# Sample attention: one page of each of four batches in a step, each batch in its own quarter of the array's columns

## The chip, the cores and the metric

The kernel runs on one core of a Trainium2 chip. The metric is the device time of one execution in microseconds (us), the median of several runs.

## The reference

One decoder layer is computed for two groups of tokens that share all weights: a prompt of 512 tokens, and a sample group of 8 batches with 4 new tokens each (32 tokens). The layer is a half-step feed-forward block, a mixer of a state-space branch (S5) and a sparse attention branch, and a second half-step feed-forward block. The change touches the attention of the sample group only:

```
# per batch b of 8: 4 queries, 8 heads of 64; past of 1024 keys = 8 pages of 128, found through page_table
score = indexer(q_idx, k_idx)                      # over 1024 + 4 keys
idx   = top_k(score, 256)
s     = q . k[idx] / 8 + bias[bucket(distance), head]
out   = softmax(s) @ v[idx]                        # then @ w_att_proj, gated by sigmoid(gate_att)
```

The keys and values of the past lie in pages of a pool in HBM, one page being 128 keys by 512 numbers in f32 (256 KB). The kernel does not gather the 256 chosen keys. It computes scores for all 1056 columns (1024 past keys and 32 new ones), adds a large negative number where a key is not chosen, and multiplies the resulting probabilities with all the values.

## The kernel before, in words

Each engine has its own instruction stream, written out by hand, and the streams meet only at semaphores. TensorE ("PE") does all matmuls and transposes. A transpose is called a turn below. PSUM has eight banks of 512 f32 columns; `ps[:, b, :]` is bank b.

The sample attention stands between the end of the prompt's attention and the projection of both. It works in two groups g of four batches. A batch has 32 rows (8 heads by 4 queries), so the four batches of a group fill the 128 partitions of PSUM: batch 4g + c has the partitions 32c to 32c + 31. The output partitions of a matmul tell which quarter of the array's columns it uses. A stationary operand is here 128 rows (or, for the new tokens, 32) by 32 columns.

**K phase of a group.** Eight steps i = 0 to 7. A step takes four pages of keys, 1 MB, which are two steps a batch. `k_turn(g, i)` (L1009) turns the four pages with 16 transposes of 128x128 into banks 3 to 6. ScalarE (L1406) copies banks 3 and 4 and VectorE (L1917) banks 5 and 6 into `pgT`, which has two buffers. `k_score(g, i)` (L1018) multiplies the step's keys with the batch's queries, which lie in `qbd` (block-diagonal over heads, four blocks j of 128 rows): four matmuls of 128x32 by 128x512, all into the same 32 partitions, accumulated over j. After each second step, four small matmuls (L1022) make the scores against the 32 new tokens. The order on TensorE is turn i, score i - 1, and after the steps 2, 3, 5 and 6 one block `ga_half` of another computation, the attention gate's projection (16 passes through the helper's line L555), which was put there as filling. Two more such blocks follow the last score. `k_turn(g, i)` waits until both copies of step i - 1 are done, since the banks are single; `k_score(g, i)` waits until those of step i are done.

**Softmax.** VectorE adds the bias and takes the maximum, ScalarE makes the exponentials (L1411), TensorE turns them (L1054, L1055), ScalarE copies them to `ptS` (L1416, L1417): `ptS[:, k, :]` holds the 128 keys of page k of all four batches, in 128 columns.

**V phase of a group.** Eight steps again; a step has four pages of values, used as they are: four matmuls (L1062) of 128x32 by 128x512 into the 32 partitions of one batch in bank 5. After each second step one matmul (L1066) adds the values of the new tokens. After the steps 4 and 5 stands a `ga_half`. VectorE then scales the result (L1927), and TensorE gathers it by token (through L555).

**Pages.** There are four slots `kpage[r]` of four pages each; step i uses slot i % 4. Two queues load them: SyncE ("SP") issues pages 0 and 1 of a slot, GpSimd ("POOL") pages 2 and 3, in the order K steps 0 to 7, V steps 0 to 7 of group 0, then of group 1 (`page_load`, L425). Each load waits on the semaphore `kv_used`, which counts steps done: in the K phase VectorE raises it once a step is turned, in the V phase TensorE does with a step's last matmul. The page number is read from the page table in SBUF just before each DMA.

**After the stage.** SyncE loads w_att_proj (L530, four blocks of 512 KB into the memory of the page slots) once the seventh V step of group 1 is done, and then w_out (L538). TensorE needs all of w_att_proj for the projection (through L555), which follows on the gathering of the result. The gate's weights are loaded on ScalarE's queue (L1389), two blocks ahead.

Of the kernel before, what the change touches and what calls it, by code (L numbers as in the profile page):

```python
# [34 lines left out]
P = 128  # L35
D = 1024
DK = D // P
SEQ, NB, NS = 512, 8, 4
NT = SEQ + NB * NS
# [63 lines left out]
def build(nc, t, out):  # L103

    ctx = ExitStack()
    with ctx:
        def sb(name, shape, dt=F32):
            return ctx.enter_context(nc.sbuf_tensor(name, shape, dt))

        def sem(name):  # L110
            return ctx.enter_context(nc.semaphore(name))
# [16 lines left out]
        qbd = sb("qbd", [P, 4, NB, HEADS * NS])  # L128
        ident = sb("ident_sb", [P, P])
# [9 lines left out]
        pt_sb = sb("pt_sb", [1, NB * NPAGE], I32)  # L139
        ps = ctx.enter_context(nc.psum_tensor("ps", [P, 8, 512], F32))  # L140
# [22 lines left out]
        ktok, vtok = kvtok[:, 0], kvtok[:, 1]  # L163
        qT, kT = qkT[:, 0], qkT[:, 1]
# [55 lines left out]
        def v(k):  # L220
# [20 lines left out]
        kpage = [[wflat[:, a:a + 512] for a in (1024, 1536, 3392, 3904)], [biasmem[:, 512 * k:512 * k + 512] for k in range(4)],  # L241
                 [biasmem[:, 512 * k:512 * k + 512] for k in range(4, 8)], [wflat[:, a:a + 512] for a in (0, 512, 2368, 2880)]]
# [7 lines left out]
        pgT = uv[:, :, :].rearrange("p a n -> p (a n)")[:, 0:4096].rearrange("p (b j n) -> p b j n", b=2, j=4)  # L250
        sms = big[:, base:base + NKEY]
        pes = big[:, base + 1056:base + 1056 + NKEY]
        ptS = big[:, base + 2112:base + 2112 + 9 * P].rearrange("p (k n) -> p k n", k=9)
# [32 lines left out]
        s = {n: sem(n) for n in (  # L286

            "gain_row_in", "par_in", "sample_const_in",
            "kidx_in", "bias_in", "att_w_in", "shift_out", "toep_in", "u_out", "u_in", "kidx_out", "kv_out", "res_out",

            "mm_done", "evac",

            "unit_done", "hi_done", "lo_done", "ffn_ev", "silu_done", "acth_done", "act_ready",

# [125 lines left out]
        def page_load(eng, first, src, g, c, i, r):  # L420

            eng.wait_ge(s["kv_used"], i * 4 + (16 * g + 8 * c + r + 1))
            for k in range(first, first + 2):
                pg = eng.value_load(pt_sb[0:1, bass.ds(i * 16 + (32 * g + 4 * r + k), 1)], min_val=0, max_val=src.shape[0] - 1)
                eng.dma_start(kpage[r][k], src[bass.ds(pg, 1), :, :].rearrange("a p d -> p (a d)")).then_inc(kv_in[first // 2][r], 16)  # L425

        def page_loads(eng, first):
# [123 lines left out]
        def _(pe):  # L551
# [130 lines left out]
            for h in range(2):  # L682
                ins = pe.matmul(ps[:, 6 + h, :], ones[0:1, :], gain_row[:, 512 * h:512 * h + 512], start=True, stop=True)
# [18 lines left out]
            for k in range(2):  # L702
                ins = pe.matmul(ps[0:HEADS, 6 + k, 0:320], relb, ohp[0:NBKT, 320 * k:320 * k + 320], start=True, stop=True)
            ins.then_inc(s["shift_mm"], 1)
            for c in range(2):
                ins = pe.transpose(ps[:, 5, P * c:P * c + P], s0raw[:, c, :], ident[:])
# [3 lines left out]
            for r in range(8):  # L710
                c, g4 = r // 4, r % 4
# [7 lines left out]
                for q in range(4):  # L719
                    ins = pe.transpose(ps[:, (r + 2) % 8, P * q:P * q + P], wb[:, c, 4 * g4 + q, :, :].rearrange("p t j -> p (t j)"), ident[:])  # L720
# [21 lines left out]
            for r in range(4):  # L742
                if r >= 2:
                    pe.wait_ge(s["lag_kernels_out"], r - 1)
                for q in range(4):
                    gp = 4 * r + q
                    for c, y in enumerate((yre, yim)):
                        for h in range(2):
                            sl = slice(64 * h, 64 * h + 64)
                            ins = pe.matmul(ps[0:16, 4 + 2 * (r % 2) + h, P * q:P * q + P], bbar[sl, c, gp, :], y[sl, gp, 0:CH, :],  # L750
                                            start=(c == 0), stop=(c == 1), skip_group_check=True)
# [12 lines left out]
            for h in range(IH):  # L764
                ins = pe.transpose(ps[:, 6, 32 * h:32 * h + 32], qis4[:, h, :, :].rearrange("p r d -> p (r d)"), ident[0:32, 0:32])
# [36 lines left out]
            for q in range(4):  # L802
                for g4 in range(4):
                    gp = 4 * q + g4
                    for h in range(2):
                        for c in range(2):
                            ins = pe.matmul(ps[64 * h:64 * h + 64, 2 * q + c, UC * g4:UC * g4 + UC], gb[:, c, gp, 64 * h:64 * h + 64],
                                            uch[:, 2 * gp + h, :], start=True, stop=True)
# [55 lines left out]
            for c in range(2):  # L864
                pe.transpose(ps[:, 0, P * c:P * c + P], fin_s[:, c, :, :].rearrange("p b g -> p (b g)"), ident[:])
                ins = pe.transpose(ps[0:GP, 0, 256 + P * c:384 + P * c], fin_p[:, c, :], ident[:])
# [30 lines left out]
            for both in range(NB // 2):  # L897
# [7 lines left out]
                if both % 2:  # L905
                    g = both // 2
                    pe.wait_ge(s["sample_relu"], g + 1)
                    for k, (c0, c1) in enumerate(cols):
                        ins = pe.matmul(ps[0:32, 5 + k, 0:c1 - c0], wsel[:, g, :], rls[:, c0:c1], start=(g == 0), stop=(g == 1))
# [3 lines left out]
            for b, (c0, c1) in enumerate(cols):  # L913
                ins = pe.matmul(ps[:, b, 0:c1 - c0], rbexp, ohs[:, c0:c1], start=True, stop=True)
# [84 lines left out]
            def k_turn(g, i):  # L999
                n = 8 * g + i  # L1000
                for half in range(2):
                    pe.wait_ge(kv_in[half][i % 4], 32 * (4 * g + i // 4 + 1))
                if i:

                    pe.wait_ge(s["k_out_act"], n)
                    pe.wait_ge(s["k_out_dve"], n)
                for j in range(4):
                    for k in range(4):
                        ins = pe.transpose(ps[:, 3 + j, P * k:P * k + P], kpage[i % 4][k][:, P * j:P * j + P], ident[:])  # L1009
                    ins.then_inc(s["k_turned"], 1)  # L1010

            def k_score(g, i):
                n = 8 * g + i
                b, q = 4 * g + i // 2, slice(32 * (i // 2), 32 * (i // 2) + 32)
                pe.wait_ge(s["k_out_act"], n + 1)
                pe.wait_ge(s["k_out_dve"], n + 1)
                for j in range(4):
                    ins = pe.matmul(ps[q, i % 2, :], qbd[:, j, b, :], pgT[:, n % 2, j, :], start=False, stop=(j == 3), skip_group_check=True)  # L1018
                ins.then_inc(s["k_scored"], 1)
                if i % 2:  # L1020
                    for j in range(4):
                        ins = pe.matmul(ps[q, 2, 0:32], qbd[:, j, b, :], kT[:, j, SEQ:NT], start=False, stop=(j == 3), skip_group_check=True)  # L1022
                    if i == 7:
                        ins.then_inc(s["sample_scores"], 1)

            def ga_half(m):

# [7 lines left out]
            for g in range(2):  # L1035
                if g:
                    pe.wait_ge(s["sample_biased"], g)
                    pe.wait_ge(s["sample_probs_out"], g)
                    pe.wait_ge(s["sample_values_out"], g)
                for k, (c0, c1) in enumerate(cols):  # L1040
                    pe.matmul(ps[:, k, 0:c1 - c0], tok_row[:, g, :], sels[:, c0:c1], start=True, stop=False, skip_group_check=True)
                for i in range(8):
                    k_turn(g, i)
                    if i:
                        k_score(g, i - 1)
                    if i in GA_AFTER_K:
                        ga_half(8 * g + GA_AFTER_K.index(i))
                k_score(g, 7)
                ga_half(8 * g + 4)
                ga_half(8 * g + 5)  # L1050
                pe.wait_ge(s["ga_ev"], 8 * g + 6)
                pe.wait_ge(s["sample_exp"], g + 1)
                for k in range(NPAGE):
                    pe.transpose(ps[:, 6 + k // 4, P * (k % 4):P * (k % 4) + P], pes[:, P * k:P * k + P], ident[:])  # L1054
                pe.transpose(ps[0:32, 5, 0:P], pes[:, PAST:NKEY], ident[:]).then_inc(s["sample_probs_turned"], 1)  # L1055
                pe.wait_ge(s["sample_probs_out"], g + 1)
                for i in range(8):
                    q = slice(32 * (i // 2), 32 * (i // 2) + 32)
                    for half in range(2):
                        pe.wait_ge(kv_in[half][i % 4], 32 * (4 * g + 2 + i // 4 + 1))  # L1060
                    for k in range(4):
                        ins = pe.matmul(ps[q, 5, :], ptS[:, 4 * (i % 2) + k, q], kpage[i % 4][k], start=(i % 2 == 0 and k == 0),  # L1062
                                        stop=False, skip_group_check=True)
                    ins.then_inc(s["kv_used"], 1)
                    if i % 2:
                        ins = pe.matmul(ps[q, 5, :], ptS[0:32, 8, q], vtok[0:32, 4, :], start=False, stop=True, skip_group_check=True)  # L1066
                        if i == 7:
                            ins.then_inc(s["sample_values"], 1)
                    if i in GA_AFTER_V:
                        ga_half(8 * g + 6 + GA_AFTER_V.index(i))  # L1070

            pe.wait_ge(s["sample_values_out"], 2)
            for j in range(4):
                ins = acc(ps[:, 6, 32 * j:32 * j + 32], [(osel[:, g, P * j:P * j + P], row_tok[:, g, :]) for g in range(2)])
# [5 lines left out]
            for i in range(DK):  # L1080
                if i >= 2:
                    pe.wait_ge(s["att_ev"], i - 1)
                for h in range(2):
                    ins = acc(ps[:, 4 * (i % 2) + h, 0:HALF], [(attw[k][:, P * i:P * i + P], attT[:, k, h * HALF:(h + 1) * HALF]) for k in range(4)])
# [13 lines left out]
            for k in range(5):  # L1098
                m = P if k < 4 else 32
                ins = pe.matmul(ps[0:m, 0, k:k + 1], running[3][:, P * k:P * k + m], ones[:, 0:1], start=True, stop=True)  # L1100
# [898 lines left out]
```

## Time and profile before

| | |
|---|---|
| median of 3 runs | 1613.44 us (1612.92 to 1614.85) |
| profiled execution | 1611.19 us |
| its span | 1609.5 us |
| TensorE busy | 95% of the span |
| VectorE, ScalarE, GpSimd busy | 38%, 28%, 16% |
| DMA | 148.00 MB, mean 92 GB/s |

The profile is of one execution. Times in it are microseconds from the start of the span. "PE" is TensorE's matmuls, "PEld" its weight loads, "DVE" VectorE, "ACT" ScalarE, "POOL" GpSimd, "SP" SyncE; a "q" behind a name means its sequencer or queue. The ends of matmuls are modelled, so spacings of starts tell more than durations. PEclk is the clock that TensorE was granted, as a share of 2.4 GHz.

### The profile page before, as it was taken

What the parts mean: (1) busy time and instruction counts of PE and PEld (TensorE: products, weight loads), DVE (VectorE), ACT (ScalarE), POOL (GpSimd) and SP (SyncE); (2) the same over time, 40 slices, a digit from 0 to 9 for tenths busy, and PEclk for the clock granted to TensorE, in tenths of its full rate; (3) what the DMA queues carried; (4) which work ended last, traced back from release to release, by engine and by line L of the source; (5) the groups of instructions that cost most, each with busy time, mean ns of one, the idle gap of its engine ahead of it and who ended that gap; (6) DMA issues with size and microseconds to landing.
All of it is one profiled execution on the core that took longest, in us unless ns stands there. A gap on an engine that the chain in (4) does not pass through costs nothing. (4 is left out here: it accounts for less than half of the span.)

```text
span 1609.5 us, 26811 instructions
## 1 busy us (share of the span) xinstructions
PE 1535.1 (95%) x10350; PEld 1314.5 (82%) x10350; DVE 608.5 (38%) x957; ACT 452.6 (28%) x647; POOL 263.7 (16%) x458
## 2 busy tenths in 40 slices
PE   7999999999899899899998999999999999999996
PEld 6999999999867677577666544635899999999996
DVE  3333343333522574155553101102454343343344
ACT  4332222122402201354543110110243222221234
POOL 3000000882003096011333111110000000000000
PEclk9999999999989999999999999999999999999998
DMA  9522323322215621721114446433233233223321
GB/s 135 143 83 79 88 82 92 89 82 72 68 23 104 107 63 17 145 62 43 53 53 148 153 138 202 144 133 105 56 89 92 79 92 92 82 88 92 87 66 61
DMA packets 228744, 148.00 MB, mean 92 GB/s; under 512 B 29730, under 2 KB 211818, under 8 KB 228667
## 3 DMA queue, kind: packets, MB, share of 16 engines
q1 hardware_dynamic: 195904, 118.06, 25.2%
q0 software_dynamic: 7088, 19.65, 5.3%
q10 hardware_dynamic: 25674, 9.25, 3.5%
q8 instruction: 51, 0.84, 0.2%
q14 instruction: 27, 0.21, 0.0%
HBM read 139.62 MB, written 6.12 MB: 91 GB/s over the span
## 5 line engine op out<-in xcount | busy, mean ns | idle before, releaser
L1597 DVE TENSOR_TENSOR w_low<-wraw,w_high 128x1024 fp32r<-128x1024 f32 x144 | 178.9, 1243 | 320.3 <-ACT w_high L1129 320.3
L575 PE MATMUL ps<-hn_high,w_high 128*128 128x272 f32 x1408 | 292.6, 289 | 2.9 <-DVE w_low L1597 2.9
L575 PE MATMUL ps<-hn_high,w_low 128*128 128x272 f32 x1408 | 292.4, 289 | 0.0
L575 PE MATMUL ps<-hn_low,w_high 128*128 128x272 f32 x1408 | 291.3, 288 | 0.0
L1129 ACT ACTIVATE w_high<-wraw 128x1024 fp32r<-128x1024 f32 x144 | 152.4, 1060 | 447.7 <-PE ps L575 443.7
L575 PEld LDWEIGHTS ps<-hn_high,w_high 128*128 128x128 f32 x1408 | 222.6, 189 | 3.1 <-issue 3.0
L575 PEld LDWEIGHTS ps<-hn_low,w_high 128*128 128x128 f32 x1408 | 222.4, 189 | 0.0
L575 PEld LDWEIGHTS ps<-hn_high,w_low 128*128 128x128 f32 x1408 | 220.7, 190 | 0.0
L575 PE MATMUL ps<-act_high,w_high 128*128 128x272 f32 x832 | 173.5, 290 | 5.3 <-DVE w_low L1597 3.5
L575 PE MATMUL ps<-act_high,w_low 128*128 128x272 f32 x832 | 172.8, 289 | 0.0
L575 PE MATMUL ps<-act_low,w_high 128*128 128x272 f32 x832 | 172.2, 288 | 0.0
L575 PEld LDWEIGHTS ps<-act_high,w_high 128*128 128x128 f32 x832 | 131.1, 189 | 6.3 <-issue 3.9
L575 PEld LDWEIGHTS ps<-act_low,w_high 128*128 128x128 f32 x832 | 131.1, 189 | 0.0
L575 PEld LDWEIGHTS ps<-act_high,w_low 128*128 128x128 f32 x832 | 130.6, 190 | 0.0
L1488 POOL TENSOR_TENSOR kvtok<-qkT,apow 128x256 f32<-128x256 f32 x68 | 51.2, 783 | 261.8 <-DVEq L1781 253.9
L555 PE MATMUL ps<-wslot,hn 128*128 128x256 f32 (+3 forms) x416 | 85.0, 369 | 1.1 <-ACT uv L1294 1.1
L555 PEld LDWEIGHTS ps<-wslot,hn 128*128 128x128 f32 (+1 forms) x416 | 66.7, 179 | 19.2 <-issue 6.2
L555 PE MATMUL ps<-uv,wslot 128*128 128x272 f32 x256 | 65.5, 399 | 5.3 <-ACT sg L1368 5.3
L555 PEld LDWEIGHTS ps<-uv,wslot 128*128 128x128 f32 x256 | 46.1, 190 | 23.4 <-issue 15.9
L940 PE MATMUL ps<-hn,wslot 128*128 128x272 f32 x256 | 65.0, 399 | 0.0
L555 PE MATMUL ps<-hn,big 128*128 128x272 f32 x256 | 62.9, 399 | 1.0 <-ACT qkT L1394 0.5
L555 PEld LDWEIGHTS ps<-hn,big 128*128 128x128 f32 x256 | 47.3, 190 | 17.6 <-issue 6.7
(328 smaller groups left out, 1746.4 us busy)
## 6 DMA issues: line engine op xcount, KB each, us to landing
wraw<-in_w_ffn_in SPq DMA_DIRECT2D x88, 512.0 KB, 3.9
wraw<-in_w_ffn_out SPq DMA_DIRECT2D x32, 512.0 KB, 3.9
wslot<-in_w_in SPq DMA_DIRECT2D x16, 512.0 KB, 4.0
wraw<-in_w_ffn_out SPq DMA_DIRECT2D x16, 384.0 KB, 3.4
wslot<-in_w_in SPq DMA_DIRECT2D x4, 1024.0 KB, 6.1
wslot<-in_cache_k POOLq DMA_DIRECT2D x16, 256.0 KB, 3.9
wslot<-in_w_s_glu SPq DMA_DIRECT2D x16, 256.0 KB, 3.0
wslot<-in_cache_k SPq DMA_DIRECT2D x16, 256.0 KB, 4.0
```

The source lines that it names most:

```text
L555: ins = pe.matmul(dst, a, b, start=(k == 0), stop=(k == len(pairs) - 1), **kw)
L575: ins = pe.matmul(ps[:, bank + h, 0:HALF], a[:, w_at, k, :], x[:, lo_at(k) if x is x_lo else k, h * HALF:(h + 1) * HALF], start=(k == 0 an ...
L940: ins = pe.matmul(ps[:, 4 * slot + h, 0:HALF], slot_block(slot, k), hn[:, k, h * HALF:(h + 1) * HALF], start=(k == 0), stop=(k == DK - 1), ...
L1129: act_e.activation(wh[:, j % 2, :, :], wraw[:, j, :, :], ACT.Copy).then_inc(s["hi_done"], 1)
L1488: ins = pool.tensor_tensor(o, a, b, ALU.mult)
L1597: return dve.tensor_tensor(o, a, b, op)
```

## The change

A step now takes page i of each of the four batches of the group, in place of four pages of one batch. The page number is read from another place of the page table (L424). The number of pages, steps, loads and semaphores stays. In `k_score` each of the four blocks j has now four matmuls of 128x32 by 128x128, one for each batch, into four different sets of 32 partitions. In the V phase the four matmuls of a step go to four different sets of 32 partitions, with 512 columns as before. The matmuls of the new tokens stand together behind the last step of the phase. `tile_position` names the quarter of the array's columns.

```diff
@@ page_load
-                pg = eng.value_load(pt_sb[0:1, bass.ds(i * 16 + (32 * g + 4 * r + k), 1)], min_val=0, max_val=src.shape[0] - 1)
+                pg = eng.value_load(pt_sb[0:1, bass.ds(i * 4 + (32 * g + 8 * k + r), 1)], min_val=0, max_val=src.shape[0] - 1)
@@ k_turn (only the name of the loop's variable)
-                    for k in range(4):
-                        ins = pe.transpose(ps[:, 3 + j, P * k:P * k + P], kpage[i % 4][k][:, P * j:P * j + P], ident[:])
+                    for c in range(4):
+                        ins = pe.transpose(ps[:, 3 + j, P * c:P * c + P], kpage[i % 4][c][:, P * j:P * j + P], ident[:])
@@ k_score
-                b, q = 4 * g + i // 2, slice(32 * (i // 2), 32 * (i // 2) + 32)
...
                 for j in range(4):
-                    ins = pe.matmul(ps[q, i % 2, :], qbd[:, j, b, :], pgT[:, n % 2, j, :], start=False, stop=(j == 3), skip_group_check=True)
+                    for c in range(4):
+                        ins = pe.matmul(ps[32 * c:32 * c + 32, i // 4, P * (i % 4):P * (i % 4) + P], qbd[:, j, 4 * g + c, :],
+                                        pgT[:, n % 2, j, P * c:P * c + P], start=False, stop=(j == 3), skip_group_check=True,
+                                        tile_position=(0, 32 * c))
                 ins.then_inc(s["k_scored"], 1)
-                if i % 2:
+                if i == 7:
                     for j in range(4):
-                        ins = pe.matmul(ps[q, 2, 0:32], qbd[:, j, b, :], kT[:, j, SEQ:NT], start=False, stop=(j == 3), skip_group_check=True)
-                    if i == 7:
-                        ins.then_inc(s["sample_scores"], 1)
+                        for c in range(4):
+                            ins = pe.matmul(ps[32 * c:32 * c + 32, 2, 0:32], qbd[:, j, 4 * g + c, :], kT[:, j, SEQ:NT], start=False,
+                                            stop=(j == 3), skip_group_check=True, tile_position=(0, 32 * c))
+                    ins.then_inc(s["sample_scores"], 1)
@@ V phase
                 for i in range(8):
-                    q = slice(32 * (i // 2), 32 * (i // 2) + 32)
                     for half in range(2):
                         pe.wait_ge(kv_in[half][i % 4], 32 * (4 * g + 2 + i // 4 + 1))
-                    for k in range(4):
-                        ins = pe.matmul(ps[q, 5, :], ptS[:, 4 * (i % 2) + k, q], kpage[i % 4][k], start=(i % 2 == 0 and k == 0),
-                                        stop=False, skip_group_check=True)
+                    for c in range(4):
+                        q = slice(32 * c, 32 * c + 32)
+                        ins = pe.matmul(ps[q, 5, :], ptS[:, i, q], kpage[i % 4][c], start=(i == 0), stop=False, skip_group_check=True,
+                                        tile_position=(0, 32 * c))
                     ins.then_inc(s["kv_used"], 1)
-                    if i % 2:
-                        ins = pe.matmul(ps[q, 5, :], ptS[0:32, 8, q], vtok[0:32, 4, :], start=False, stop=True, skip_group_check=True)
-                        if i == 7:
-                            ins.then_inc(s["sample_values"], 1)
+                    if i == 7:
+                        for c in range(4):
+                            q = slice(32 * c, 32 * c + 32)
+                            ins = pe.matmul(ps[q, 5, :], ptS[0:32, 8, q], vtok[0:32, 4, :], start=False, stop=True, skip_group_check=True,
+                                            tile_position=(0, 32 * c))
+                        ins.then_inc(s["sample_values"], 1)
```

## Rows read from the trace of the kernel before

**Rows 1.** The page's part 1: busy time, share of the span, instructions.
```profile
PE 1535.1 (95%) x10350; PEld 1314.5 (82%) x10350; DVE 608.5 (38%) x957; ACT 452.6 (28%) x647; POOL 263.7 (16%) x458
```

**Rows 2.** The page's part 4: the chain's shares of the span by line.
```profile
PE ps L575 28%; PE ps L555 6%; PE ps L1018 4%; PE ps L1062 3%; PE ps L1009 2%; PE ps L1066 0%; DVE sg L1597 0%; PE ps L609 0%; DVE uv L1917 0%; PE ps L1054 0%; ACT big L1416 0%; PE ps L1022 0%; DVE act_low L1597 0%; ACT L1440 0%; DVE w_low L1597 0%
```

**Rows 3.** Chain in order of time, second K phase: start us, us, what, passes.
```profile
988.94 2.99 PE ps L1009 x16
...
992.06 1.24 DVE uv L1917
993.30 0.14 issue
...
996.81 3.55 PE ps L1018 x8
...
1005.81 0.25 PE ps L1022 x8
...
1045.11 6.98 PE ps L1018 x16
...
1052.34 3.88 PE ps L555 x16
```

**Rows 4.** The same chain, second V phase and what follows.
```profile
1063.58 7.05 PE ps L1062 x16
1070.63 0.97 PE ps L1066 x2
...
1079.56 3.55 PE ps L1062 x8
1083.11 3.86 PE ps L555 x16
...
1102.34 0.98 PE ps L1066 x2
...
1103.42 0.70 DVE sg L1597
...
1104.17 2.33 PE ps L555 x16
...
1106.88 32.36 PE ps L555 x128
```

**Rows 5.** L807 by stretch: length, PE and PEld busy (records), PEclk, DMA share, GB/s.
```profile
556.00:558.00 2.00, 2.00 (x38) 2.00 (x36) 0.50 0.17 54
559.60:560.80 1.20, 1.20 (x45) 1.20 (x43) 1.00 0.00 0
```

**Rows 6.** Timeline of TensorE, index scores of a pair of batches.
```profile
672.14 0.67 PE L892 MATMUL ps<-wslot,qis 32*32 32x128 f32 x24
```

**Rows 7.** All engines by stretch; the last three numbers: PEclk, DMA share, GB/s.
```profile
1070.00:1080.00 10.00, 10.00 (x24) 2.14 (x23) 0.00 (x0) 0.00 (x0) 2.65 (x6) 1.00 0.82 280
1100.00:1110.00 10.00, 8.76 (x31) 5.19 (x30) 0.98 (x2) 0.00 (x0) 0.00 (x0) 0.78 1.01 329
```

**Rows 8.** Timeline of SyncE's queue and GpSimd, first reload of the second V phase.
```profile
1068.06 1.52 SPq L425 DMA_DIRECT2D wslot<-in_cache_v  x2
...
1069.84 0.54 POOL L425 DMA_DIRECT2D wslot<-in_cache_v  x1 [0.80 <-issue]
```

**Rows 9.** DMA issues from 1069.2: count, KB each, median us to landing.
```profile
wslot<-in_cache_v SPq DMA_DIRECT2D x1, 256.0 KB, 4.4
```

**Rows 10.** Timeline of SyncE's queue at the end of the stage.
```profile
1098.94 0.34 SPq L530 DMA_DIRECT2D wslot<-in_w_att_proj  x1
...
1099.33 1.37 SPq L530 DMA_DIRECT2D biasmem<-in_w_att_proj  x3
```

**Rows 11.** DMA issues there, the last two blocks of w_att_proj.
```profile
biasmem<-in_w_att_proj SPq DMA_DIRECT2D x2, 512.0 KB, 5.6
```

**Rows 12.** Timeline of TensorE; in brackets the idle time before, and its releaser.
```profile
1142.75 0.49 PE L575 MATMUL ps<-act_high,w_high 128*128 128x272 f32 x2 [3.53 <-DVE w_low L1597]
```

**Rows 13.** L575 in the stretch after that gap, columns as in rows 5.
```profile
1143.20:1146.50 3.30, 3.30 (x17) 3.30 (x16) 0.50 0.80 218
```

## The prediction

> **What bounds the kernel now.** Read the page's first part, then its fourth. TensorE is busy for 1535.1 us of a span of 1609.5 [rows 1]; the chain that ended last consists of its lines, and two of the lines that the diff rewrites, L1018 and L1062, are its third and fourth longest [rows 2]. No other engine passes 38%. Then read the chain in order of time through the sample attention of the second group; the first one repeats it. In the K phase (from 988.94 to 1052.34, 63.4 us) turns of a step, scores of the step before and blocks of the gate projection (L555) follow one another; only once does the engine wait, 1.5 us for the VectorE copy L1917 of step 0 [rows 3]. In the V phase (1063.58 to 1103.32, 39.7 us) there is no wait at all [rows 4]: the pages are always there. So time taken from TensorE's stream in these phases comes off the end, until a copy or a page is late.
>
> The profiled execution took 1611.19 us by the clock of the runs (1609.5 is its span), 2.25 below their median of 1613.44. I subtract from the first and add 2.25 at the end. "The same" means within 0.2%, 3.2 us, which is about what can be told from no change.
>
> **What the change does to a pass.** A matmul in f32 stands in the trace as two passes: L1018 has 8 records for the 4 matmuls of a step. One step takes 3.55 us, two in a row 6.98 [rows 3]; the second adds 3.43, so a pass of 512 columns takes 0.428 us (0.107 per 128 columns) and a change of shape 0.12. All passes of a step now use one quarter of the array's columns. Afterwards a K step has 32 passes of 128 columns in the place of 8 of 512, in four quarters in turn, and a V step the same 8 passes of 512, two in each quarter. The columns streamed are the same; everything hangs on whether quarters stream side by side.
>
> The trace shows that for halves. L807 writes 64 columns at partitions 0 or 64, with all 128 rows in use, 72 moving columns, so 0.060 us a pass by the rate above. At full clock 45 of its passes touch a stretch of 1.20 us [rows 5]: 2.7 us of streaming, two at a time. At the lower clock 38 touch 2.00 us, where each streams for 0.120: again two. The weight loads of 64 columns kept up. For quarters there is L892 (32 rows by 32 columns): 24 passes of 128 columns, 2.57 us of streaming, lie in 0.67 us [rows 6], at least four at a time, and batches in neighbouring column quarters join without a gap. Four quarters over all 128 rows are not shown. The bounds are two at once (0.053 us per 128 columns) and four at once (0.027). I take four, since the halves lose nothing against their limit.
>
> **K phase, part by part.** Score of a step: 32 passes, four at a time, 8 x 0.107 = 0.86, and 0.12 for the change of shape: 0.98 against 3.55. Sixteen steps: 16 x 2.57 = 41.1 us off. L1022 (8 passes of 32 columns in 0.25 [rows 3], four times a group) becomes one run of 32; its bounds are 0.25 and 1.0 us, I take 0.5, so 1.0 off for both groups. The 3.55 us also hid something: the copies of a turned step. From the end of step 0's turns to the next turn pass 1.50 us, 1.24 of them the VectorE copy [rows 3]. Steps 2 and 5 turn without a gate block before them, and the last score has no turn before it; there 0.98 covers the copy no longer, and 0.52 is idle: 6 x 0.52 = 3.1 us given back. K phases together: 39.0 off.
>
> The Trainium skill says beside this (TensorEngine Tiling (Array Packing), Performance Considerations, PSUM Bottleneck) that tiling quickens the matmuls but not the copies out of PSUM, which may then bind. By that rule alone the step would be the copy's; the rows of this case agree for three steps a group, and the gate blocks hide it in the others.
>
> **V phase, part by part.** The pages of steps 0 to 3 were fetched during the K phase; those of 4 to 7 are asked for as a slot comes free. The first four steps take 4 x 0.86 = 3.4 us. Slot 0 is free at 0.86 plus a tail of some 0.16, T + 1.0 (T is the phase's start). Its four pages before: the phase began at 1063.58, step 0 ended 3.6 later, SyncE issued the first page at 1068.06 and the second some 1.2 later, GpSimd its second at 1069.84 [rows 8]; SyncE's second took 4.4 us to land [rows 9], thus at 1073.7, 6.5 after the release. I take 6.15, between that and the 5.8 of the first group by the same reading. Step 4 can start at T + 7.15 instead of 3.4: a new stall of 3.7 us. From there steps 4 to 7 (3.44), three changes of shape (0.36), two gate blocks (2 x 3.86 [rows 4]) and the values of the new tokens, now four matmuls side by side in 0.86 + 0.12 in place of 4 x 0.97 [rows 4]: the phase ends at T + 19.7. Before: 39.7. Both groups: 40.0 off.
>
> Do the later slots hold that up? A slot is 1.05 MB. The queues moved 280 GB/s at a busy share of 0.82 and 329 at 1.01 [rows 7], so about 335 when full: 3.1 us a slot. They are full at T + 7.2, 10.3, 13.4 and 16.6; the engine comes to them at 7.2, 12.1, 17.0 and 17.8, the gate blocks being between. Hidden. The first K slots of group 1 follow on the same queues (SyncE and GpSimd take them in order) at T + 19.7, 22.8, 25.9 and 29.0; the next K phase, starting 1.6 us after the V phase's end with turns at half clock, comes to them at about 21.3, 25.8, 30.7 and 37: hidden, by 1.6 us at the least. Each GpSimd issue takes some 1.2 us, 2.4 a slot, under 3.1.
>
> **What becomes late at the end.** SyncE asks for w_att_proj once V step 6 of group 1 is done, at 1098.94, the last of four blocks at about 1100.3 [rows 10]; these last ones took 5.6 us or more [rows 11], so all are there at 1106.3, and the projection begins at 1106.88 [rows 4]. It is hidden by 0.6 us. Afterwards only 0.86 + 0.98 (step 7, tokens) and the 3.6 from 1103.32 on lie between, 5.4 against 7.4: 2.0 us exposed. Given back: 2.0.
>
> **The clock.** A gap of 3.53 us on TensorE at 1142.75 was followed by a stretch at half clock, 0.50 from 1143.20 to 1146.50 [rows 12, 13]: 3.4 us, 1.7 of them lost. The two new stalls of 3.7 us look alike. The fall at 990 has its cause, whatever it is, around the phases' border and stays. I charge 2 x 1.7 = 3.4; the ends are 0 and, for a stretch twice as long each time, 6.8.
>
> **Sum.** 39.0 + 40.0 - 2.0 - 3.4 = 73.6 us. 1611.19 - 73.6 = 1537.6, and with the 2.25: **1540 us**. With the bounds of L1022 (0.5 us a group), the reload (5.8 to 6.5, twice), the clock (0 to 6.8) and w_att_proj (1 to 3): 1533 to 1548.
>
> **The rivals.**
> (a) Only two quarters stream at once, as far as rows 5 go. Score 1.71 + 0.12 = 1.83, 1.72 off a step, 27.5; copies hidden; L1022 1.0; V: four steps 6.8, reload at 1.9 + 6.15 = 8.0, then 6.84 + 0.36 + 7.72 + 1.83 = T + 24.8, 14.9 off each; the stall of 1.2 is too short to count for the clock; w_att_proj 0.3 late. 58.0 off: **1555**. For it: no row with more than two full-height streams. Against: L892.
> (b) Four at once, but rounds don't abut, each some quarter longer: score 1.2, values 1.08 a step. K loses 16 x 0.22 less the idle that it fills (6 x 0.22), 2.2; V per group 0.2 + 4 x 0.22 + 0.22, 2.6 for both: **1545**.
> The Trainium skill (TensorE: Matmul & The Clock Gate, Part 3, Measured speedup) gives 2.38 times for three column tiles, where three is the limit; its sum would be near (b). No run here has shown that ratio.
> (c) The clock: with TensorE streaming for less and idling more, it falls two or three times more and for 6.8 us each. Each costs 3.4: four of them in all instead of my 3.4: 10 more, **1550**. For: it fell at 990 after a gap under 1 us and a V phase of narrow passes. Against: it stayed full through both K phases.
> (d) Quarters don't overlap and every change of quarter drains the array, at the 0.12 of a change of shape. A K step has 16 changes, a V step 4: 16 x 16 + 16 x 4 = 320, 38 us, less 4 or so for the grouped token passes: **1647**, slower than before. It decides from 0.01 us a change (320 x 0.01 is the 3.2 us of no change), if nothing overlaps. Against: L807 changes its half every four passes and reaches twice the rate.
> (e) No overlap and no drain, the diff only reorders: **1613**.
>
> **How the numbers follow.** Forecast 60%, (a) 12, (b) 12, (c) 9, (d) 4, (e) 3. Faster by over 0.2%: 93%; within: 3%; slower: 4%. The likeliest case spans 1533 to 1548; the range goes on to (a) with its own reload bound: 1532 to 1557.
>
> **What would show it.** Steps 0 and 1 of a V phase in 1.7 us, against 7.05 now, confirm four streams; 3.4 means (a); 7 means (e). L1018's 32 passes in about 1 us, then TensorE idle for VectorE L1917 at steps 2 and 5, some 0.5 us each. In each V phase a gap of 3.5 to 4 us before step 4, ended by a page, and perhaps a half-clock stretch after it; without that stretch the time is 1537. A wait of 2 us for w_att_proj. Wrong would be: single passes of the four quarters starting one after the other, or idle time before steps 5 to 7, which would mean that the queues give less than 335 GB/s.

## The result, and the profile after

The changed kernel takes 1541.13 us (median of 4 runs, 1538.80 to 1544.07) against 1614.14 for the one before (4 runs, 1612.92 to 1615.52): a ratio of 0.9551, 95% interval 0.9534 to 0.9568, 73 us less. The forecast was 1540, in 1532 to 1557.

The profiled execution took 1543.36 us. Part 1 of its page, to be read against [rows 1]: TensorE has 384 more matmul records and 78.9 us less busy time, the other engines are nearly as they were.

```profile
PE 1456.2 (94%) x10734; PEld 1307.1 (85%) x10734; DVE 608.9 (39%) x957; ACT 452.9 (29%) x647; POOL 262.1 (17%) x458
```

The chain in order of time through the second K phase (start us, us, what, passes), against [rows 3]:

```profile
955.67 2.65 PE ps L1009 x16
...
958.46 1.24 DVE uv L1922
...
963.63 1.24 DVE uv L1922
964.86 0.14 issue
965.00 1.94 PE ps L1009 x16
966.94 1.01 PE ps L1018 x32
967.95 3.86 PE ps L555 x16
...
997.03 1.23 DVE uv L1922
998.26 0.14 issue
998.40 1.06 PE ps L1018 x30
999.46 0.30 PE ps L1025 x30
999.76 3.88 PE ps L555 x16
```

A score step of 32 passes takes 1.01 us where 8 passes took 3.55. VectorE's copies, which TensorE waited for only at step 0, now stand in the chain at steps 2, 5 and before the last score as well. The phase runs from 955.67 to 999.76, 44.1 us in place of 63.4.

The second V phase and what follows, against [rows 4]; "DMA" is the flight of a transfer for which the chain waits. From here on, T is the start of a V phase, as in the prediction.

```profile
1011.00 1.73 PE ps L1065 x8
...
1015.37 4.30 DMA wslot<-in_cache_v
1019.67 0.14 issue
1019.81 1.06 PE ps L1065 x8
1020.88 3.86 PE ps L555 x16
1024.74 1.00 PE ps L1065 x8
...
1029.60 1.04 PE ps L1065 x8
...
1031.99 6.43 DMA biasmem<-in_w_att_proj
1038.43 0.14 issue
1038.56 31.28 PE ps L555 x128
```

The phase ends at 1032.4, 21.4 us after its start, in place of 39.7. Two waits are new. One is for GpSimd's second page of the first reloaded slot: step 4 begins at 1019.81, where the matmuls of the first four steps were through at 1016.3. The other is for the last block of w_att_proj. The timeline of TensorE shows the first kind in the first group of batches; in brackets the idle time and its releaser:

```profile
941.45 0.64 PE L1065 MATMUL ps<-wslot,big 128*32 128x512 f32 x4 [3.57 <-DMA wslot<-in_cache_v]
```

From the first matmul of the stage to the first of the projection it is 233.7 us before (873.16 to 1106.88) and 161.6 after (876.94 to 1038.56): 72.1 off. The rest of the difference between the two spans, 4.3 us in the other direction, lies outside the stage. The stage begins 3.8 us later (876.94 against 873.16), in code that the change does not touch; ahead of it the clock was at half for some 36 us in place of 24 in these two traces.

### The profile page after: what moved, and what is told of

It reads as the page before. It is cut to its first block and busy times, and to the rows that moved or that the text cites. A ratio compares the mean times of both kernels' runs of the same rounds, so it can differ in the third digit from the quotient of the medians.

```text
span 1541.7 us, 27579 instructions
## 1 busy us (share of the span) xinstructions
PE 1456.2 (94%) x10734; PEld 1307.1 (85%) x10734; DVE 608.9 (39%) x957; ACT 452.9 (29%) x647; POOL 262.1 (17%) x458
## 5 line engine op out<-in xcount | busy, mean ns | idle before, releaser
L575 PE MATMUL ps<-hn_high,w_high 128*128 128x272 f32 x1408 | 292.3, 289 | 2.9 <-DVE w_low L1602 2.9
L575 PE MATMUL ps<-hn_high,w_low 128*128 128x272 f32 x1408 | 291.5, 288 | 0.0
L575 PE MATMUL ps<-hn_low,w_high 128*128 128x272 f32 x1408 | 291.2, 288 | 0.0
L575 PEld LDWEIGHTS ps<-hn_high,w_high 128*128 128x128 f32 x1408 | 221.8, 189 | 3.1 <-issue 3.0
L575 PEld LDWEIGHTS ps<-hn_low,w_high 128*128 128x128 f32 x1408 | 222.1, 189 | 0.0
L575 PEld LDWEIGHTS ps<-hn_high,w_low 128*128 128x128 f32 x1408 | 220.6, 189 | 0.0
L575 PE MATMUL ps<-act_high,w_high 128*128 128x272 f32 x832 | 174.3, 291 | 5.3 <-DVE w_low L1602 3.5
L575 PE MATMUL ps<-act_high,w_low 128*128 128x272 f32 x832 | 173.1, 290 | 0.0
L575 PE MATMUL ps<-act_low,w_high 128*128 128x272 f32 x832 | 172.7, 289 | 0.0
L575 PEld LDWEIGHTS ps<-act_high,w_high 128*128 128x128 f32 x832 | 131.6, 190 | 6.3 <-issue 3.9
L575 PEld LDWEIGHTS ps<-act_low,w_high 128*128 128x128 f32 x832 | 131.7, 190 | 0.0
L575 PEld LDWEIGHTS ps<-act_high,w_low 128*128 128x128 f32 x832 | 130.8, 190 | 0.0
L555 PE MATMUL ps<-hn,wslot 128*128 128x272 f32 (+1 forms) x272 | 61.2, 383 | 0.0
```

The lines of the kernel that those rows point to most:

```text
L555: ins = pe.matmul(dst, a, b, start=(k == 0), stop=(k == len(pairs) - 1), **kw)
L575: ins = pe.matmul(ps[:, bank + h, 0:HALF], a[:, w_at, k, :], x[:, lo_at(k) if x is x_lo else k, h * HALF:(h + 1) * HALF], start=(k == 0 an ...
```

## The experiments

Each was timed beside the kernel before on its own chip; ratios are against that, with 95% intervals.

**The changed kernel again, and each half alone.** e0 is unchanged. e1 and e2 choose the page number by phase:

```diff
+        def page_at(c, i, g, r, k):          # c == 0: keys, c == 1: values; e1 (e2 has it the other way round)
+            return i * 4 + (32 * g + 8 * k + r) if c == 0 else i * 16 + (32 * g + 4 * r + k)
...
-                pg = eng.value_load(pt_sb[0:1, bass.ds(i * 4 + (32 * g + 8 * k + r), 1)], ...
+                pg = eng.value_load(pt_sb[0:1, bass.ds(page_at(c, i, g, r, k), 1)], ...
# and the V phase's loop (e2: k_score) as in the kernel before
```

> The changed kernel once more, beside its variants. Theory (its two levels of 1538.9 and 1543.7 us come from where the clock of TensorE falls outside the stage that was changed, the stage itself always takes the same): 1539 to 1544 us, and the sample attention from its first matmul (L1044) to the first of the projection takes 161.6 us within 1 us, as in the first profile. Rival (the two levels lie in the stage, in the page loads or in half-clock stretches at the V phases): the stage differs by 3 us or more.

Measured: 1539.59 us (1538.96 to 1542.86), 0.9541 (0.9516 to 0.9566). The stage took 162.0 us (873.85 to 1035.89). The theory held for the stage as a whole: it repeats within 0.4 us, while the spans of the two profiles, 1541.7 and 1538.0, differ by 3.7, so that difference lies outside it. Its parts don't repeat. The V phases took 23.5 and 21.1 us where the first profile has 21.6 and 21.4, and the second K phase 41.6 in place of 44.1: a half-clock stretch fell on the first V phase's wait (937.4 to 944.4) and none on the start of the second K phase.

> Only the K phases take a page of each batch; the V phases and their page numbers are as before. Theory (the phases' gains are independent, each from its own matmuls in four quarters): the K phases take 43 to 44 us each in place of 62 to 63, the V phases 39.7, w_att_proj is not waited for; 38.4 us off, 1575.7 us (1573 to 1579). On the clock: the half-clock stretch that the changed kernel has at the start of each V phase comes from the sparser K phase before it, so it is here too (about 932 and 1011 there). Rival (the stretch comes from the V phase itself, its stall included): the clock stays full at the V phases' start.

Measured: 1573.75 us (1572.81 to 1576.33), 0.9752 (0.9727 to 0.9776). The gain, 40 us by the ratio, agrees with the 38.4 named, within its interval. The K phases took 44.9 and 41.6 us, the V phases 39.7 each, and w_att_proj is not waited for. On the clock the rival held. The two V phases, by stretch (length, busy us of PE, PEld, DVE, ACT and POOL with their records, PEclk, DMA share, GB/s), are at full clock throughout:

```profile
929.00:971.00 42.00, 40.05 (x107) 13.11 (x105) 0.57 (x1) 1.97 (x4) 7.89 (x15) 1.00 0.63 195
1023.00:1065.00 42.00, 40.22 (x109) 13.27 (x107) 0.41 (x1) 1.97 (x4) 4.30 (x8) 1.00 0.40 133
```

> Only the V phases take a page of each batch; the K phases are as before. Theory: V phases of about 20 to 21.5 us in place of 39.7, with a stall of 3.5 us before step 4 in each for the reloaded pages, and some 3 us of waiting for w_att_proj; 33.7 us off, 1580.4 us (1577 to 1583). If the half-clock stretch at a V phase's start comes from the sparser K phase, it is absent here, step 0 and 1 take 1.7 us, and the V phases are 1 us or more shorter (19.7 us, as first forecast), 1578. Rival: the stretch is there, or one follows the stall at step 4.

Measured: 1579.82 us (1576.87 to 1585.89), 0.9792 (0.9758 to 0.9826), 33.6 us by the ratio. The V phases took 22.2 and 21.9 us, a little more than named, and w_att_proj was waited for. The half-clock stretch is there, and here it follows the stall before step 4 (953.6 to 958.0, 1049.5 to 1053.6), the columns as above:

```profile
958.00:961.20 3.20, 3.20 (x11) 1.30 (x12) 0.00 (x0) 0.00 (x0) 1.20 (x3) 0.50 0.95 360
1053.50:1056.70 3.20, 3.09 (x11) 1.22 (x12) 0.00 (x0) 0.00 (x0) 1.57 (x3) 0.50 0.95 334
```

So a sparser K phase alone does not bring the stretch (e1), and the one at the stall comes without it (e2). A stretch at the very start of a V phase, as in the changed kernel, shows in neither: it may need both halves, and its cause is not shown. The two halves' savings add up to the whole: 40 + 33.6 against 73 to 74.

**Is it the quarters, or the shorter passes?** e3 is the kernel before, its score matmuls cut in four:

```diff
-                    ins = pe.matmul(ps[q, i % 2, :], qbd[:, j, b, :], pgT[:, n % 2, j, :], ...
+                    for k in range(4):
+                        ins = pe.matmul(ps[q, i % 2, P * k:P * k + P], qbd[:, j, b, :], pgT[:, n % 2, j, P * k:P * k + P], ...
```

> The kernel before, with each score matmul of 512 columns cut into four of 128, all in the same quarter of the array. Theory (the gain comes from quarters that stream side by side, not from shorter passes or their order): a score step keeps its 3.5 us (32 passes of 0.107 to 0.109), the total is 1614 to 1616 us. Rival (shorter passes overlap by themselves, loads and matmuls better interleaved): a score step near 1 to 2 us, 1575 to 1590.

Measured: 1613.84 us, 1.0001 (0.9984 to 1.0019). The chain in order of time has this for a step:

```profile
888.35 3.61 PE ps L1019 x32
```

The same 32 passes of 128 columns take 3.61 us in one quarter and 1.01 in four. The gain is the quarters'.

**The order of the passes.** Three kernels change the order of the 16 matmuls of a score step and nothing else:

```diff
-                for j in range(4):
-                    for c in range(4):
+                for c in range(4):                                                                        # e4
+                    for j in range(4):
+                for j, c in [(2 * jj + j, c) for jj in range(2) for c in range(4) for j in range(2)]:     # e9
+                for j, c in [(j, 2 * cc + c) for cc in range(2) for j in range(4) for c in range(2)]:     # e10
```

> The changed kernel with the two loops of a score step swapped: all four blocks j of one batch (8 passes in one quarter), then the next batch. Theory (each quarter streams what is queued for it, whatever stands in front for another quarter, as the two halves of L807 did, four passes at a time): a score step stays at 1.0 to 1.2 us, the total within 3 us of the changed kernel's 1541. Rival (passes start in program order, so that the quarters overlap only where the order alternates): a quarter's 8 passes run nearly alone, a step takes 2.5 to 3.4 us, the total is 1565 to 1578 us.

Measured: 1559.27 us (1553.08 to 1563.86), 0.9654 (0.9632 to 0.9676), between the theory's time and the rival's. The chain of e4, and a stretch of its step beside it in the next fence (length, PE and PEld busy, PEclk, DMA share, GB/s):

```profile
886.84 2.39 PE ps L1018 x32
```

```profile
886.90:889.10 2.20, 2.20 (x32) 2.06 (x31) 1.00 0.56 168
```

2.39 us a step: neither the whole overlap nor nearly none. In the starts of the single passes, read from the step at 882.5, the first of the second quarter comes 0.466 us after the step's first, just behind the fifth pass of the first quarter (0.460). My first reading of this was that a pass may overtake at most three unstarted ones, whatever their quarter. e9 and e10 were made for that.

> The changed kernel, score step in the order: for each half of the blocks j, for each batch, two matmuls (4 passes of one quarter before the next quarter). Theory (a pass can start once its quarter is free and no more than three passes stand unstarted before it in program order; this gives 20 x 0.109 = 2.18 us for the order by batch, where the trace shows 886.90 to 889.07, and 0.87 for the changed kernel's): 11 x 0.109 = 1.20 us, with the change of shape 1.32 a step, 3 us more in all (16 x 0.31 less 6 x 0.3 of idle time filled), 1544 us. Rival (only two quarters stream at once unless every matmul changes its quarter): 1.74 + 0.12 = 1.86 a step, 1551.5 us. Second rival (each change of quarter within a step costs a fixed time, (2.16 - 0.87) / 3 where three changes are made): seven changes, 3 us a step or more, 1565.

Measured: 1540.46 us (1538.77 to 1544.52), 0.9549 (0.9524 to 0.9575). From the chain:

```profile
885.71 1.05 PE ps L1018 x32
```

1.05 us, where that reading asked for 1.32 and the rivals for more. It fell: the passes of all four quarters start within 0.04 us, and the last quarter's first one then has nine unstarted in front of it.

> The changed kernel, score step in the order: batches 0 and 1 in turn for all four j, then batches 2 and 3. Theory (three unstarted passes may be overtaken): 14 x 0.109 = 1.53 us, 1.65 a step, 7 us more in all, 1548 us; in the trace the second pair's first passes start while the last few of the first pair still wait. Rival (two at once, no overlap between the pairs): 1.86 a step, 1551.5 us. Rival (one change of pair costs 0.43): 1.30 + 0.12 = 1.42 a step, 1545.

Measured: 1548.21 us (1544.57 to 1554.01), 0.9607 (0.9580 to 0.9633). The median total was as forecast, the step was not, so the total confirms nothing:

```profile
885.39 1.47 PE ps L1018 x32
```

The step was forecast as 1.65 us by that reading; the nearest forecast is the second rival's, a fixed cost for one change of pair, with 1.42 a step and 1545 in all (the profiled execution took 1544.57). But a fixed cost for each change is what e9 speaks against, with seven changes of quarter in a step and 1.05 us.

What fits all of them is a limit by quarter: one pass streams and three wait for it, and a fifth holds up everything behind it, other quarters too. In e4 three further quarters come 0.467 us apart, which makes 3 x 0.467 + 8 x 0.109 = 2.27; measured are 2.30 from the first start to 0.109 behind the last. In e10 the second pair starts 0.473 us in, together 0.473 + 0.87 = 1.34, measured 1.38. In e9 and in the changed kernel no quarter ever has a fifth pass waiting while another quarter's first is behind it: 0.95 and 0.92. It also fits L807, with four passes a half. This rule was formed after the last of these runs, and no run was made to refute it: it is fitted, not shown.

**The new waits.** e5 moves the gate blocks of the V phase, e6 asks for w_att_proj block by block, e7 has both and puts a block before the last score of a K phase; e8 is e7 without the edit of e6.

```diff
-        GA_AFTER_K, GA_AFTER_V = (2, 3, 5, 6), (4, 5)
+        GA_AFTER_K, GA_AFTER_V = (2, 3, 5, 6), (3, 4)                      # e5, e7, e8
...
-            sp.wait_ge(s["kv_used"], 4 + 31)
             for k in range(4):
+                sp.wait_ge(s["kv_used"], 4 + (29, 30, 30, 31)[k])         # e6, e7
                 sp.dma_start(attw[k], t["w_att_proj"][0, P * k:P * k + P, :]).then_inc(s["att_w_in"], 16)
...
-                k_score(g, 7)
                 ga_half(8 * g + 4)
+                k_score(g, 7)                                             # e7, e8
                 ga_half(8 * g + 5)
```

> The changed kernel with the two gate blocks of a V phase after the steps 3 and 4 in place of 4 and 5, so that the first lies where TensorE now waits 3.1 to 4.8 us for the first reloaded slot. Theory (the V phase is then bound by the page queues: in the first profile the four slots landed 8.8, 11.7, 14.6 and 17.2 us after its start, so step 7 cannot begin before 17.2): the phase ends at 17.2 + 0.86 + 1.0 = 19.1 in place of 21.5, 2.4 us off in each, 1536 us; the idle time moves from before step 4 to before the steps 6 and 7. Rival (the stall is all there was and the later slots are early enough): 3.5 to 4 us off in each, 1533 to 1534 us. Second rival (the idle time filled brings no gain since it only moves): 1541.

Measured: 1537.09 us (1531.50 to 1544.48), 0.9529 (0.9501 to 0.9557). The V phases took 19.2 and 19.1 us (931.49 to 950.66, 1006.74 to 1025.88) as the theory said. The first one's chain now waits for the last slot instead, before step 7:

```profile
942.85 5.62 DMA wslot<-in_cache_v
948.47 0.14 issue
948.60 1.06 PE ps L1065 x8
```

With the wait before step 4 covered the page loads bind, and only 2.4 of the 3.5 us are gained. From the first slot's release on, every link of this chain is an issue of GpSimd, which takes 1.2 to 1.3 us a page without a pause; the first and the last of its eight in the V phase:

```profile
933.90 0.54 POOL L425 DMA_DIRECT2D wslot<-in_cache_v  x1 [13.43 <-PE ps L1065]
...
942.85 0.54 POOL L425 DMA_DIRECT2D wslot<-in_cache_v  x1 [0.69 <-issue]
```

That is 2.6 us a slot, where the slots landed one per 2.8. The DMA engines were busy at a share of 0.93 to 1.04 meanwhile (936 to 948), so they too were near their limit; which of the two sets the 2.8 is not shown, since no run gave SyncE a larger part of the pages. The total alone could not tell this from the rivals, since its interval is too wide.

> The changed kernel; SyncE issues each block of w_att_proj as soon as the slot under it is free (after the V steps 4, 5, 5 and 6 of group 1), in place of all four after step 6. Theory (3.1 to 3.3 us of waiting for it before the projection are on the path, and V's last pages have landed by then or are ahead in the queues): the wait goes and the projection begins 0.4 us after the copy before it, 3.2 us off, 1537.5 to 1538 us. Rival (the blocks take bandwidth from the last pages, steps 6 and 7 come later by what is gained): 1541.

Measured: 1537.96 us (1535.32 to 1540.45), 0.9522 (0.9509 to 0.9534). Between the gathering of the result and the projection the chain now has only a copy and two gaps below 0.05 us:

```profile
1036.77 0.30 DVE kvtok L1935
1037.07 0.04 issue
1037.12 31.30 PE ps L555 x128
```

TensorE's gap there is 0.38 us, as in the kernel before, where the changed kernel has 3.25. No wait came before the steps 5 to 7, so the rival fell. The trace shows this and not the total, whose ratio can't be told from that of e0. Both V phases took 23.6 us here, the first one too, ahead of any block of w_att_proj: the clock was at half for 6.8 us in each.

> The changed kernel with the edits of e5 and e6 and a third: the first of the two gate blocks that follow the last score of a K phase stands before that score, where TensorE waits 0.5 us for the copies. Theory: 4.8 us from the V phases, 3.2 from w_att_proj less up to 1.5 since its blocks now compete with the last reloaded slot, 1.0 us in each K phase (0.5 of the copies' wait and 0.5 of the wait for the gate block's own copy, both now covered): 8 to 10 us off, 1531 to 1533 us. Rival (less than the sum, the page queues bind and everything put before them waits there): 5 us off, 1536.

Measured: 1536.55 us (1531.60 to 1537.00), 0.9506 (0.9490 to 0.9521): the rival's time, and not the theory's 1531 to 1533. The second V phase took 22.2 us (1006.04 to 1028.2) where e5 had 19.1; step 7 waited 2.9 us for its slot:

```profile
1017.42 6.86 DMA wslot<-in_cache_v
1024.29 0.14 issue
1024.42 1.94 PE ps L1065 x8
1026.36 1.90 PE ps L1071 x8
1028.36 0.70 DVE sg L1602
```

The page took 6.86 us where e5's took 5.62 and 5.59, with early blocks of w_att_proj in the queues: 1.3 us. The other 1.8 are the clock's, which was at half from 1024.2 and doubled the last steps. So of the 3 us more the queues account for less than half in this trace, and that the early blocks delayed the page rests on this one phase.

> The changed kernel with the gate blocks of a V phase after the steps 3 and 4, and the first block after a K phase put before its last score; w_att_proj asked for as in the changed kernel. Theory (the blocks of w_att_proj, asked for early, took bandwidth from the last reloaded slot of the second V phase and cost 3 us there, while behind step 6 of this shorter phase they are hidden by the wait for that slot): both V phases take 19.1 us, a K phase 1.0 less, w_att_proj is not waited for by more than 1 us; 1541.1 - 4.8 - 2.1 - 2.5 = 1531.7 us (1530 to 1535). Rival (the difference between these variants is the clock's, not the queues'): 1536.5 as the three edits together.

Measured: 1533.34 us (1531.83 to 1533.98), 0.9502 (0.9483 to 0.9521), the fastest of all, 6 to 8 us below the changed kernel by the medians (e0 and the first runs). The V phases took 19.1 and 18.7 us. The end of the second and what follows:

```profile
1014.38 5.38 DMA biasmem<-in_cache_v
1019.76 0.14 issue
1019.89 1.10 PE ps L1065 x8
...
1022.37 6.49 DMA biasmem<-in_w_att_proj
1028.85 0.14 issue
1028.99 32.02 PE ps L555 x128
```

Of w_att_proj 1.9 us are still waited for (0.9 more than expected). The total is in the theory's range of 1530 to 1535. That e8 beats e7 by its median agrees with the theory too, but is not shown: the intervals of the two ratios overlap, two of e7's five executions took under 1533 us, and its traced one was the slowest of the five, with the half clock in it.

## Why the prediction was right, point by point

The time came out right for the reason given, four quarters at once. Two of its smaller terms were off and made up for each other.

- **The bound.** TensorE's stream in the two phases was on the path all through: 78.9 us less of it made 72.1 us in the stage.
- **Four quarters at once.** Right, and what everything hung on. The step took 1.01 us, forecast 0.98; rivals (a), (d) and (e) fell, (d) also by e9, where fewer changes of quarter bring nothing. The rounds abut: four passes every 0.109 us. So (b) fell too. The Trainium skill (TensorE: Matmul & The Clock Gate, Part 3, Measured speedup) has 2.38 times for three column tiles. No run here used three; with four, e3 against the changed kernel is 3.61 to 1.01, 3.6 times, 0.9 of the limit where the page's figure is 0.8 of its own.
- **The copies that come into view.** Forecast 0.52 us at three places of a K phase; the gaps in the trace are 0.49 to 0.51 there, at steps 2, 5 and before the last score. The Trainium skill's warning of PSUM copies (TensorEngine Tiling (Array Packing), PSUM Bottleneck) agrees with these three gaps. L1025's run took 0.30 for 0.5. K phases together: 38.2 us off (62.3 to 43.4, 63.4 to 44.1), forecast 39.0.
- **V phases.** Forecast T + 19.7 and 1.7 for the clock in each, 21.4; measured 21.6 and 21.4. That they agree so well is luck, for two terms inside were off and made up for each other: the clock's place and the reload. The half-clock stretch was to fall behind the stall and cost 1.7; in the first profile it falls with the phase's start:

```profile
932.80:936.10 3.30, 3.30 (x20) 0.85 (x16) 0.50 0.03 6
```

   (L1065 by stretch, columns as for e4.) Steps 0 and 1 take twice their time, but only step 0's share is on the path, since the rest passes inside the wait: slot 0 is free at T + 1.8 in place of 1.0, 0.8 us. The reload gives as much again: its pages land 7.0 us later where 6.15 was taken. So step 4 starts at T + 8.9, not 7.15; from there to the end 12.6 us were forecast and 12.7 measured. The reload was sized too small in every trace: over the 20 V phases with the new order it is 6.4 to 7.6 us, at full clock too, and the forecast's bounds were 5.8 to 6.5. The phase as a whole was 21.1 to 23.8 us, 22.7 on average, in the 14 where the code of the V phase is the changed kernel's (with e0, e2, e4, e6, e9, e10), so the first profile's two are at the short end.
- **The reload stall** before step 4 was forecast as 3.7 us and is 3.57 and 3.47, later than forecast at both its ends; over the same 14 V phases it is 3.1 to 5.1. No wait came before the steps 5 to 7, as forecast. The slots of the first phase landed 8.8, 11.7, 14.6 and 17.2 us after T, one per 2.8 us, some 375 GB/s, so the 335 of the forecast was low.
- **w_att_proj.** Forecast 2.0 us exposed; the projection starts 6.1 us after the V phase's end in place of 3.6, so 2.5 to 2.6. e6 takes it away whole.
- **The clock, rival (c).** In the first profile it did not fall more often than charged, once in each V phase for 3.4 us. That is not the rule: in 6 of the 14 V phases named below the half clock lasts 6.8 us in all, which is the charge's upper end. The forecast's argument against (c), that the clock stayed full through both K phases, was a misreading: in the trace before it is at half from 870.0 to 877.0 and from 989.4 to 996.4, in the first turns of each, as in the changed kernel (874.6 to 881.6, 956.6 to 963.6). Over all traces, the 14 V phases with a wait above 3 us before step 4 (the changed kernel twice, e0, e2, e4, e6, e9, e10, two each) all have a half-clock stretch inside, of 3.4 or 6.8 us; of the 12 without one (before, e1, e3, e5, e7, e8) only e7's second has, from 1024.2, behind its 2.9 us wait. In 9 of the 14 it begins in the last two microseconds or so of the wait, which ties the two together. In the other 5 phases it begins with the phase, ahead of the wait (932.6 in the first profile), and in two of them a second one comes with the wait. None begins so in e1, e5, e7 and e8, where the code before that point is the same or nearly so; why, stays open.

The sum in the stage: 38.2 + 18.1 + 18.3 - 2.6 = 72.0 against 73.6 forecast. The bounds that the forecast lists give 1534 to 1546 and not the 1533 to 1548 that it states; nothing hangs on that.

## What to carry to other kernels

Where a matmul leaves three quarters of the columns empty, give four independent outputs their own 32 partitions each and let the instruction stream alternate between them: here that made the stream 3.6 times as fast, and between two orders with the same passes lay some 18 us (e4). Then ask what the longer stream had covered: here copies (0.5 us each), page reloads (3.5 us a phase) and a weight load (2.6 us), which could be foreseen from issue times and landing times in the trace before, the reload about 1 us too short. Filling such a gap gains only up to the next limit (e5: 2.4 of 3.5 us). An earlier load may take its bandwidth from the one that is waited for; here one phase of e7 suggests it, and e6 shows no such harm.

## What the runs showed of the hardware

- Column quarters over all 128 rows stream side by side in f32 at no loss: four passes of 128 columns start within 0.02 us, the next four 0.109 us later (0.13 after the first four of a step); weight loads of 32 columns keep up.
- A quarter seems to take one streaming pass and three waiting ones, and a fifth in a row to hold up what is behind it (fitted to these runs). 8 passes a quarter in a row: 2.39 us a step; pairs of quarters: 1.47; 4 in a row: 1.05; 2 in a row: 1.01.
- Cutting passes shorter within one quarter costs little: 32 passes of 128 columns in place of 8 of 512 added 0.06 us a step.
